# Two passes over the first weight slab in five stages of a Trainium2 kernel

## The reference, cut to what matters

```python
for l in range(DEPTH):                       # DEPTH = 2
    h = x * (1.0 + scale[:, None]) + shift[:, None]
    proj = h @ w_in[l]                       # "projection"
    ...
    y_hg = o_hg.astype(x.dtype) @ w_branch_hg[l]   # "merge": branches
    ...
```

## Time and profile before

| what | us |
| --- | --- |
| median of three runs | 4398.41 |
| lowest, highest | 4391.02, 4407.63 |
| the profiled execution, its time | 4402.04 |
| its span (first to last instruction) | 4400.3 |
| TensorE busy in it | 3834.6 (87%) |
| VectorE busy | 2376.4 (54%) |
| ScalarE busy | 1783.7 (41%) |
| GpSimd busy | 1076.5 (24%) |

### The profile page before, as it was taken

One profiled execution on the slowest core, in us unless ns is written; L12 is line 12 of the kernel. 1 busy time (PEld: TensorE's weight loads), 2 busy tenths in 40 slices (PEclk: granted clock), 3 DMA queues, 4 the chain that ended last, 5 costly groups with the idle time before them and its releaser, 6 DMA issues. The chain is left out here.

```text
span 4400.3 us, 78490 instructions
## 1 busy us (share of the span) xinstructions
PE 3834.6 (87%) x30752; PEld 2895.2 (66%) x30752; DVE 2376.4 (54%) x2958; ACT 1783.7 (41%) x2347; POOL 1076.5 (24%) x955
## 2 busy tenths in 40 slices
PE   7999888888897998989996988888787999999953
PEld 4888666666675887766665754546546777777733
DVE  4456554553663001745554652752356887888757
ACT  1111244442332111444443341532206777777734
POOL 1212113211331221221211320001004444444434
PEclk8999999888998999989887999999798999999975
DMA  6775333112423432332113313511218888798857
GB/s 230 230 229 186 125 105 136 62 45 83 134 96 122 140 119 93 114 130 85 65 39 128 128 64 123 214 41 39 109 43 350 324 307 323 295 403 345 306 213 259
DMA packets 285205, 724.13 MB, mean 165 GB/s; under 512 B 36112, under 2 KB 127888, under 8 KB 268048
## 3 DMA queue, kind: packets, MB, share of 16 engines
q1 hardware_dynamic: 224752, 396.27, 26.3%
q0 software_dynamic: 48960, 283.17, 16.9%
q10 hardware_dynamic: 11232, 40.90, 2.3%
HBM read 631.09 MB, written 168.82 MB: 182 GB/s over the span
## 5 line engine op out<-in xcount | busy, mean ns | idle before, releaser
L476 PE MATMUL ps<-s_proj_hS,s_proj_wS 128*128 128x512 f32 x3216 | 776.8, 404 | 40.4 <-POOL s_proj_wS L370 28.8
L476 PEld LDWEIGHTS ps<-s_proj_hS,s_proj_wS 128*128 128x128 f32 x3216 | 618.3, 193 | 195.0 <-issue 46.6
L3370 PE MATMUL ps<-s_exp_wS,exp_x 128*128 128x512 f32 x2208 | 540.5, 400 | 0.0
L3370 PEld LDWEIGHTS ps<-s_exp_wS,exp_x 128*128 128x128 f32 x2208 | 410.1, 189 | 92.9
L531 PE MATMUL ps<-gate_h,gate_w 128*128 128x512 f32 x1536 | 415.6, 422 | 36.3 <-PEq L154 19.3
L518 POOL TENSOR_TENSOR gate_w<-gate_raw,gate_w 128x512 fp32r<-128x512 f32 x128 | 187.0, 1463 | 819.1 <-ACT gate_w L512 818.2
L531 PEld LDWEIGHTS ps<-gate_h,gate_w 128*128 128x128 f32 x1536 | 294.6, 196 | 138.4 <-issue 51.4
L393 DVE COPY s_proj_o<-ps 128x512 f32<-128x512 f32 x66 | 45.6, 691 | 555.0 <-PE ps L476 555.0
L3308 DVE TENSOR_TENSOR s_exp_wS<-exp_gu,s_exp_wS 128x1024 fp32r<-128x1024 f32 x276 | 325.3, 1219 | 30.1 <-ACT s_exp_wS L3254 29.9
L370 POOL TENSOR_TENSOR s_proj_wS<-s_proj_w,s_proj_wS 128x1024 fp32r<-128x1024 f32 x67 | 169.0, 2523 | 673.4 <-ACT s_proj_wS L425 673.4
L3254 ACT ACTIVATE s_exp_wS<-exp_gu 128x1024 fp32r<-128x1024 f32 x276 | 286.5, 1070 | 28.6 <-DMA exp_gu<-in_w_gu_dram,s_exp_widx 17.1
(11 more groups left out here) (491 smaller groups left out, 7029.2 us busy)
## 6 DMA issues: line engine op xcount, KB each, us to landing
yrow<-keep_hT SPq DMA_DIRECT2D x92, 512.0 KB, 4.7
keep_mix<-in_w_ada_dram SPq DMA_DIRECT2D x80, 512.0 KB, 6.4
s_proj_w<-in_w_in_dram SPq DMA_DIRECT2D x66, 512.0 KB, 6.1
proj<-s_proj_o ACTq DMA_DIRECT2D x66, 512.0 KB, 2.7
gate_raw<-in_w_in_dram SPq DMA_DIRECT2D x128, 256.0 KB, 3.4
yrow<-keep_xT SPq DMA_DIRECT2D x4, 8192.0 KB, 48.5
s_rw_edge<-proj SPq DMA_DIRECT2D x34, 512.0 KB, 4.5
s_mix_sg<-gates SPq DMA_DIRECT2D x32, 512.0 KB, 3.3
```

Of the source, the lines that this page charges most:

```text
L476: mm = pe.matmul(k.ps[:, 6 + half if last else 2 * b + half, :], wS[:, b, x, t, :], hS[:, y, t, half * HALF:(half + 1) * HALF], start=(t = ...
L3370: mm = pe.matmul(k.ps[:, 2 if u % 2 == 0 else 6, :], xS[:, u % 2, h, 2 * pr + t, :], wS[:, pr, w, t, :], start=(pr == 0 and t == 0 and h + ...
```

## The change

In the first slab of the projections (first half of the tokens), of the merges (first half, branches) and of the output projection (both halves), TensorE waits only for the rounded weights, goes over all tiles with the two terms that read them, then waits for the remainder and goes over all tiles with the third term, into the same banks. All other slabs stay as they are. The core of the diff:

```diff
                 wait(pe, hi_ready, n + 1)
+                if isinstance(n, int) and n == 0:
+                    for t in range(KT):
+                        pe.wait_ge(hhi_ready, t + 1)
+                        pe.wait_ge(hlo_ready, t + 1)
+                        for y in range(2):
+                            pe.matmul(k.ps[:, 0, :], wS[:, 0, 0, t, :], hS[:, y, t, 0:HALF], start=(t == 0 and y == 0), stop=False)
+                    pe.wait_ge(lo_ready, 1)
+                    for t in range(KT):
+                        mm = pe.matmul(k.ps[:, 0, :], wS[:, 0, 1, t, :], hS[:, 0, t, 0:HALF], start=False, stop=(t == KT - 1))
+                    mm.then_inc(half_ready, 1)
                 wait(pe, lo_ready, n + 1)
...
-                for half in range(2):
+                for half in range(1 if isinstance(n, int) and n == 0 else 0, 2):
                     for t in range(KT):
-                        if isinstance(n, int) and n == 0 and half == 0:
-                            pe.wait_ge(hhi_ready, t + 1)
-                            pe.wait_ge(hlo_ready, t + 1)
...
                 pe.wait_ge(hi_ready, z + 1)
+                if m == 0:
+                    for x in range(KT):
+                        pe.wait_ge(yl_ready, x + 1)
+                        for v in range(2):
+                            pe.matmul(k.ps[:, x // 4, :], wS[:, 0, 0, x, :], yS[:, v, x, :], start=(x % 4 == 0 and v == 0), stop=False)
+                    pe.wait_ge(lo_ready, 1)
+                    for x in range(KT):
+                        mm = pe.matmul(k.ps[:, x // 4, :], wS[:, 0, 1, x, :], yS[:, 0, x, :], start=False, stop=(x % 4 == 3))
+                        if x % 4 == 3:
+                            mm.then_inc(ys_ready, 1)
+                    return
...
             for j in range(KT):
+                if j == 0:
+                    pe.wait_ge(hi_ready, 1)
+                    for half in range(2):
+                        cut = slice(half * HALF, (half + 1) * HALF)
+                        for t in range(KT):
+                            if half == 0 and t == KT - 1:
+                                pe.wait_ge(lastl_ready, 1)
+                            for y in range(2):
+                                pe.matmul(k.ps[:, half, :], wS[:, 0, 0, t, :], mS[:, y, t, cut] if t < KT - 1 else lastS[:, y, cut],
+                                          start=(t + y == 0), stop=False)
+                    pe.wait_ge(lo_ready, 1)
+                    for half in range(2):
+                        cut = slice(half * HALF, (half + 1) * HALF)
+                        for t in range(KT):
+                            mm = pe.matmul(k.ps[:, half, :], wS[:, 0, 1, t, :], mS[:, 0, t, cut] if t < KT - 1 else lastS[:, 0, cut],
+                                           start=False, stop=(t == KT - 1))
+                    mm.then_inc(o_ready, 1)
+                    continue
                 pe.wait_ge(lo_ready, j + 1)
```

More of the change, by code:

```diff
@@ L2792, in _ @@
                     for t in range(KT):
-                        if j == 0 and half == 0 and t == KT - 1:
-                            pe.wait_ge(lastl_ready, 1)
                         for x, y in TERMS:
```

## The result

| | us |
| --- | --- |
| before, median of 16 runs (lowest, highest) | 4398.74 (4389.79, 4413.74) |
| changed, median of 16 runs (lowest, highest) | 4411.49 (4400.47, 4417.90) |
| ratio, 95% interval | 1.0022 [1.0014, 1.0030] |
| span of the profiled execution, before and changed | 4400.3, 4410.4 |

The account below looks back on a forecast made before the run. VectorE's last tile bounds projections and merges, GpSimd's remainder the output projection. Projections 1.6 + 0.9 + 1.6 + 0.1, merges 1.4 + 0.3, output projection -2.4: +3.5 us on median 4398.41, so 4401.9, range 4392 to 4413.

Parts of the forecast that it names:

- upper end, +9.8: Whole kernel: all stage costs at their worst and the output projection gaining only 1.2 us.
- the gate: Projections and merges: TensorE must wait for VectorE's last activation tile, so the 2.4 us earlier projection start is worth nothing.
- Rival (b): All five starts: the weights' remainder was the true wait, each moves forward 2.4 us; -12.0 us, 4386.4; chance 0.03.
- the start is unchanged, but the stream is thinner: Merges: the clock may rise as late as 6.04 us after the start, not 2.94; up to +1.55 us more each.
- +1.4 and +0.3: Merges, layers 0 and 1: cost in us of ten matmuls left after VectorE's last tile.
- Rival (a): Stages fed tile by tile: thin first pass keeps the clock down, costing half of each further us; 4408; chance 0.15.
- +1.6 and +0.9: Projection, layer 0: +1.6 us for seven more matmuls after the last tile, +0.9 us for a later clock rise.
- The mean of three rises behind a dense start, 4.12 us: Projections: clock rise counted from the last tile by three dense starts, 2.94, 6.04 and 3.37 us.
- the bound of 6.04: Projections: latest clock rise allowed after the last tile, in us; clock term up to +1.9 in layer 0, +1.1 in layer 1.
- Layer 1's term, +1.7: Projection, layer 1: +1.6 us for seven more matmuls after the last tile, +0.1 us for the clock.
- I take the mean effect: Output projection: with the clock rising 3.37 us after the start as before, all 2.4 us of earlier start are gained.
- the other end that the prediction kept: Output projection: if the clock rises at 3014.12 whatever TensorE does, only 1.2 us is gained.

Follow-up runs that it names:

- The early start that was caught up: Kernel before, but first two projection tiles (merges: one) use rounded weights before the remainder, third term follows at once; one run, 4406.11 us, before 4397.79.
- the filled pair: Changed kernel and kernel before, each with idle matmuls in TensorE's waits in projections and merges; one run each, 4405.42 and 4401.06 us, unfilled before 4397.79.
- the projections' part alone: Kernel before with the change in the two projections only; 4408.78 us against 4403.03, ratio 1.0013 [1.0003, 1.0023].
- the kernel with slab 0 tile by tile: Kernel before, but slab 0 of the projections does both token halves for each tile; one run, 4393.31 us, before 4397.79.
- the one that has the output part too: Kernel before with projections' slab 0 tile by tile over both halves and the output projection as changed; 4389.38 us against 4401.06, ratio 0.9977 [0.9964, 0.9989].
- the changed kernel kept busy: Changed kernel with idle matmuls in TensorE's waits at the starts of projections and merges; one run, 4405.42 us, before 4397.79.

## Why the prediction was right, and where its sizes were not

The time (4401.9, range 4392 to 4413) was 10 us short; the measured 4411.49 lies in the range and within 0.5% of before, and the sign was right. The predicted +3.5 us lies below the measured interval, 6 to 13 us, and its upper end, +9.8, within it. That the range holds the time, 1.5 us below its upper end, is in part luck: it was drawn wider than the costs by the scatter of the runs, and the medians lie further apart than the costs' upper end.

**Right: the gate.** That VectorE's last tile and not GpSimd's remainder bounds four of the five starts, that an earlier first matmul there is worth nothing, and that the order leaves seven more matmuls behind it. The early start that was caught up shows the first two, the filled pair gives 1.64 us for 7 x 0.233. Rival (b), -12 us, is excluded by the first matmuls that came earlier and won nothing. The stages' gain and loss were handed on to their ends. The signs that the prediction named came too: VectorE as releaser in the projections and merges, ScalarE's rounding in the output projection, and its take 13.75 us behind the first matmul (12.8 to 14.0 stated).

**Mis-sized: the clock in the merges.** The step "the start is unchanged, but the stream is thinner" was made a bound, +1.55 us in each, and the sum took nothing of it: +1.4 and +0.3, where +2.9 and +2.0 were measured. In both layers the thin first pass ended before the clock rose, in two executions of three in layer 1 and in all three in layer 0. Rival (a), given 0.15, is what happened in three of the four stages fed tile by tile, at its price of half of each us; the five stages came to +7.5, between my +3.5 and its +9.8.

**Mis-sized: layer 0's projection.** "+1.6 and +0.9" against +3.1. The mean of three rises behind a dense start, 4.12 us, was too early for a stage whose first pass keeps TensorE busy for half of the time; 5.5, 6.3 and 6.3 us were measured (the third in the projections' part alone). The two last lie beyond the bound of 6.04 too. Layer 1's term, +1.7, was met with +1.5; there the rise came 3.5 to 4.3 us behind the last tile, hardly later than in two of the three traces with the order of before (2.3, 3.8, 3.9). Why the two layers differ with the same instructions isn't shown.

The prediction read only the last rise of the clock in these stages. In the kernel before it had been full once already, in layer 0 from 54.8 to 58.2, and had fallen again:

```profile
56.00:58.00 2.00, 0.00 (x0) 0.00 (x0) 2.00 (x1) 0.00 (x0) 2.00 (x2) 1.00 0.93 359
...
60.00:62.00 2.00, 0.00 (x0) 0.00 (x0) 1.97 (x2) 0.00 (x0) 0.38 (x1) 0.50 0.00 0
```

All three traces with the order of before have such a stretch in both layers, none of the three with two passes has it. It comes behind the first twelve matmuls, which stand in one piece from 50.44 on (rows 2) and which an earlier start pulls apart. By itself it is worth nothing: the kernel whose early start was caught up lacks it too, and its clock rose 1.8 and 2.2 us behind the last tile.

**Mis-sized: the output projection.** -2.4 us was taken and -1.5 measured at the take (the whole stage had -1.9, but the stage of before was 0.4 us longer in its trace than in the five others with its order; against those it is -1.5 too). The step that failed is "I take the mean effect": I reasoned that the rise keeps its distance from TensorE's first matmul. It didn't. In the eleven traces without idle matmuls in this stage the clock rose 9.9 to 10.5 us after the stage's start, whether the first matmul came at 4.6 (five traces) or at 7.0 (six). The extra matmuls ran at the low clock, and half of the time came back: 1.2 us, the other end that the prediction kept.

The stage's start need not be what sets the moment. The clock had last fallen about 10 us before it, and the distance from that fall to the rise is the same 20.5 us in all eleven. Before and changed (fall, and for the changed kernel the rise; the rise of before is in rows 7):

```profile
2992.00:2994.00 2.00, 0.00 (x0) 0.00 (x0) 1.97 (x2) 0.55 (x1) 0.00 (x0) 0.91 0.00 0
```

```profile
3006.00:3008.00 2.00, 0.00 (x0) 0.00 (x0) 1.93 (x3) 0.34 (x1) 0.00 (x0) 0.76 0.00 0
3026.00:3028.00 2.00, 2.00 (x7) 1.51 (x7) 0.00 (x0) 0.00 (x0) 0.84 (x1) 0.62 0.73 256
```

By the slices' means the clock fell at 2993.64 and rose at 3014.12 before, and fell at 3007.04 and rose at 3027.52 after: 20.48 us both times. With TensorE kept busy from the stage's start it rose 13.7 us behind the fall.

The Trainium skill's page "TensorE: Matmul & The Clock Gate", section "What's actually happening", says that the window behind the clock is free-running and isn't reset when a kernel starts. These traces agree in so far as the first matmul didn't set the moment. The prediction had read the page's amount of time as one that counts from the first matmul; from there to the rise it was 5.4 to 6.0 us with the early start and 3.0 to 3.5 without, so that reading failed.

**Left over.** The five stages give +7.5 us in the profiled executions, which differ by 10.1; the rest is in stages that the change doesn't touch, and they vary by more than that. The recurrent stage of layer 1 has the same instructions in each kernel and took 481.8 us in the kernel with slab 0 tile by tile and 474.0 in the one that has the output part too:

```profile
1898.10:2379.90 481.80, 415.54 (x8006) 316.10 (x8006) 230.01 (x291) 200.63 (x248) 97.66 (x57) 0.86 0.25 85
```

```profile
1898.10:2372.10 474.00, 405.92 (x8006) 307.91 (x8006) 229.78 (x291) 200.45 (x248) 97.82 (x57) 0.89 0.26 87
```

The matmuls are the same 8006, TensorE's busy time differs by 9.6 us and the mean clock by 0.03. Where in that stage the clock falls and rises depends on the execution. Against the trace of before it was 4.0 and 4.2 us longer in the two traces of the changed kernel, but also 4.4 with the early start caught up and 5.1 with slab 0 tile by tile, and 0.9 and 0.3 with the projections' part alone and with the changed kernel kept busy. Whether the change shifts it in one direction the traces can't tell. That stays open.

## What to carry to other kernels

A wait on the releasers' list is not worth its length: ask which wait ends last in the stretch, and how much work is left behind it. Where an operand arrives piece by piece, order the consumer so that the least work stands behind the last piece (here six matmuls instead of 27: -6 us a stage); splitting a term off into a second pass puts more work there (34: +1.6 us and more). Thinner work in a wait can also leave TensorE at its lower clock for the dense part that follows: it did in layer 0's projection in all three traces and in the merges in five stages of six.

## What the runs showed of the hardware

The granted clock's rise in the output projection came 9.9 to 10.5 us after the stage's start in eleven traces, whether TensorE's first matmul came at 4.6 or at 7.0 us, and 20.5 us behind the clock's last fall in all eleven. It moved to 3.7 us after the stage's start when TensorE was kept busy from there. Idle matmuls, whose results nobody reads, had the clock up before the last tile in every projection and merge in which they were tried; in the merges they are worth 1.1 us where the clock had been late (take at 1.2 us behind the last tile and not 2.3). Where they outlast the wait they cost what they overrun, 0.4 us in the output projection.
